# Rotary row swaps by shuffles on the vector engine instead of permutation matmuls on the tensor engine

## The reference

```python
# axial attention of the first block, 16 query heads of 64 on 4 key groups; pairs (i, i + 16) in each 32 rows
q = rms(q) * q_gain;  k = rms(k) * k_gain
q, k = rotate(q), rotate(k)            # x * cos + swap(x) * sin, of the 512 tokens, not of the context
# _mla_branch, 8 heads ("latent"): 64 plain rows and 32 rotary rows, pairs (i, i + 16); key rows shared by the heads
q_pe, k_pe = rotate(q_pe), rotate(k_pe)
# _diff_branch, 8 heads ("diff"): two queries and two keys of 64 rows, the first 16 of each turned, pairs (i, i + 8)
dq, dk = rotate(dq[:16]), rotate(dk[:16])
scores = q @ k.T;  weights = softmax(scores);  out = weights @ v
```

## Time and profile before

| | before |
|---|---|
| median of 3 runs | 4189.98 us (4186.84 to 4192.81) |
| span of the profiled execution | 4189.2 us |
| PE busy | 3968.2 us, 95% |
| DVE busy | 2070.7 us, 49% |
| ACT busy | 1490.1 us, 36% |
| POOL busy | 1630.0 us, 39% |
| mean granted TensorE clock | 0.968 |

### The profile page before, as it was taken

The page is one execution under the profiler, slowest core; times in us unless marked ns, Lnnn a source line. Parts: engine busy times, 40 slices in busy tenths (PEclk is TensorE's granted clock), DMA queues, the critical chain, the costliest instruction groups (busy, mean ns, idle before and its releaser), DMA issues.

```text
span 4189.2 us, 59665 instructions
## 1 busy us (share of the span) xinstructions
PE 3968.2 (95%) x20860; PEld 3354.5 (80%) x20860; DVE 2070.7 (49%) x3364; ACT 1490.1 (36%) x2420; POOL 1630.0 (39%) x2044
## 2 busy tenths in 40 slices
PE   7999988999988979999999999999989999999998
PEld 6788888999977767888777788788877777887887
DVE  5556655223347666225737723533367476235225
ACT  3212222111236543222646534322246456333222
POOL 1111123333421105566333245466642423555565
PEclk9899999999989989999999999999999999999999
DMA  5334211112110002322121122223221211322222
GB/s 187 125 123 144 79 51 51 61 65 64 61 46 26 21 11 93 98 98 96 56 70 57 51 86 96 76 96 100 96 66 41 81 51 61 100 86 77 99 95 96
DMA packets 92747, 328.31 MB, mean 78 GB/s; under 512 B 10240, under 2 KB 12544, under 8 KB 92544
## 3 DMA queue, kind: packets, MB, share of 16 engines
q1 hardware_dynamic: 90928, 323.61, 23.3%
q10 hardware_dynamic: 1616, 1.90, 0.2%
HBM read 323.38 MB, written 2.10 MB: 78 GB/s over the span
## 4 chain that ended last, share of the span: by engine, by line
issue 61%; POOL 30%; PE 8%; DVE 1%; POOLq 1%; ACT 0%; DVEq 0%
POOL Wl L259 30%; PE psum L1142 3%; PE psum L1143 3%; PE psum L1144 3%; POOLq L254 0%; POOLq L256 0%; DVE S L1990 0%; DVE M L2168 0%; PE psum L1209 0%; DVE X L1990 0%; DVE X L2124 0%; PE psum L1199 0%; DVE X L2185 0%; POOLq L259 0%; ACT hand L380 0%
## 5 line engine op out<-in xcount | busy, mean ns | idle before, releaser
L259 POOL TENSOR_TENSOR Wl<-raw,Wh 128x256 fp32r<-128x256 f32 x2040 | 1629.8, 829 | 2552.9 <-ACT Wh L370 2552.5
L370 ACT ACTIVATE Wh<-raw 128x1024 fp32r<-128x1024 f32 x510 | 540.0, 1059 | 1689.9 <-PE psum L1144 1664.3
L1142 PE MATMUL psum<-Hh,Wh 128*128 128x512 f32 (+1 forms) x2704 | 1037.9, 384 | 50.2 <-DVEq L2033 17.0
L1143 PE MATMUL psum<-Hl,Wh 128*128 128x512 f32 (+1 forms) x2704 | 1018.3, 377 | 0.0
L1144 PE MATMUL psum<-Hh,Wl 128*128 128x512 f32 (+1 forms) x2704 | 1017.0, 376 | 0.0
L1142 PE MATMUL psum<-Gh,Wh 128*128 128x512 f32 (+3 forms) x2032 | 751.1, 370 | 17.5 <-DVEq L2033 7.9
L1144 PE MATMUL psum<-Gh,Wl 128*128 128x512 f32 (+3 forms) x2032 | 745.7, 367 | 0.0
L1143 PE MATMUL psum<-Gl,Wh 128*128 128x512 f32 (+3 forms) x2032 | 745.3, 367 | 0.0
L1142 PEld LDWEIGHTS psum<-Hh,Wh 128*128 128x128 f32 x2704 | 520.5, 192 | 157.6 <-issue 52.1
L1144 PEld LDWEIGHTS psum<-Hh,Wl 128*128 128x128 f32 x2704 | 520.1, 192 | 71.4
L1143 PEld LDWEIGHTS psum<-Hl,Wh 128*128 128x128 f32 x2704 | 521.0, 193 | 67.9 <-issue 1.3
(11 more groups left out here) (345 smaller groups left out, 4702.9 us busy)
## 6 DMA issues: line engine op xcount, KB each, us to landing
raw<-in_wstream SPq DMA_DIRECT2D x510, 512.0 KB, 3.4
stage<-in_ada SPq DMA_DIRECT2D x80, 512.0 KB, 4.3
M<-in_ada SPq DMA_DIRECT2D x16, 512.0 KB, 5.9
X<-in_xT SPq DMA_DIRECT2D x1, 2048.0 KB, 14.1
out<-X SPq DMA_DIRECT2D x8, 256.0 KB, 2.0
X<-in_ctxT SPq DMA_DIRECT2D x1, 1024.0 KB, 9.2
M<-in_memT ACTq DMA_DIRECT2D x1, 1024.0 KB, 5.6
M<-in_axial ACTq DMA_DIRECT2D x1, 512.0 KB, 3.5
```

The lines of the kernel that those rows point to most:

```text
L259: pool.tensor_tensor(Wl[:, s, c], raw[:, s, c], Wh[:, s, c].bitcast(F32), ALU.subtract).then_inc(w_low, 1)
L370: act.activation(Wh[:, s], raw[:, s], ACT.Copy).then_inc(v["w_high"], 1)
L1142: pe.matmul(dst, a[0], b[0], start=first, stop=False)
L1143: pe.matmul(dst, a[0], b[1], start=False, stop=False)
```

## The change

The three permutation matrices are gone, and so are all 62 matmuls with them, with the PSUM tile, the bank and the wait that each took. DVE makes the swap itself, with `stream_shuffle`, which permutes the partitions inside each 32, from SBUF to SBUF; then it multiplies the result by the sine table, in SBUF too. The signs of the sine table now are zero in rows that aren't rotary, since the shuffle moves those rows as well. PE's waits for raw values move from in front of the swaps to in front of the transposes that still need them.

```diff
-CONST_COLS = 6 * P + 4
+CONST_COLS = 3 * P + 4
+SWAPPED = {n: [i ^ n for i in range(32)] for n in (8, 16)}
...
 # axial attention, PE
-    def rotated_keys():
-        pe.wait_ge(v["keys_scaled"], keys_scaled.next())
-        exact(P, SEQ, rot0, k32[:, X0:TOK])
-
-    def rotated_queries(t):
-        exact(P, SEQ, rot0, q_raw[t])
...
-                if u == 5:
-                    rotated_keys()
                 if u == 6:
-                    rotated_queries(0)
                     square_sums(1)
...
 # latent attention, PE
         if more:
-            rotated(2 if before else 3)
             keys_and_values()
-        else:
-            pe.wait_ge(v["raw_done"], counts.raw_done.next())
+        raw_values_taken(3 if h < 2 else 2)
         turned_values(h)
...
     from_tokens()
-    twin_rotated(0)
-    twin_rotated(1)
-    pe.wait_ge(v["raw_done"], counts.raw_done.next())
+    raw_values_taken(1)
     turned_values(1)
...
 # diff attention, PE
         scores(4 * h + 3)
-        if more:
-            rotated(0)
-            rotated(1)
         turned_weights(4 * h + 2)
...
 # axial attention, DVE
     def turn(x):
-        b = look()
-        tt_last(b, S0[:], psum[:, b, :], sinA, ALU.mult)
+        do(dve.stream_shuffle(S0[:], x, SWAPPED[16]))
+        tt(S0[:], S0[:], sinA, ALU.mult)
         tt(x, x, cosA, ALU.mult)
         tt(x, x, S0[:], ALU.add)
...
 # latent attention, DVE
+    swapped = v["diag"][rope].rearrange("p b q -> p (b q)")
     def rotate():
-        b = look()
-        tt(S0[rope, :], psum[rope, b, :], sinM[rope, :], ALU.mult)
-        free(b)
+        do(dve.stream_shuffle(swapped, S0[rope, :], SWAPPED[16]))
+        tt(S0[rope, :], swapped, sinM[rope, :], ALU.mult)
         tt(S0[rope, :], S0[rope, :], S1[rope, :], ALU.add)
         dve.sem_inc(v["turned_ready"], 1)
...
 # diff attention, DVE
-    def turned_part(b):
-        tt_last(b, turned, halves(psum[:, b, :]), sinD, ALU.mult)
+    def turned_part(c):
+        do(dve.stream_shuffle(turned, X[:, 2 * c:2 * c + 2, 0:CTX], SWAPPED[8]))
+        tt(turned, turned, sinD, ALU.mult)
...
         if more:
-            turned_part(look())
+            turned_part(0)
         low_weights(1, weights_bank)
         combine(4 * h + 3)
-        if more:
-            key = look()
         low_weights(2, look())
         if more:
             rotate(0)
-            turned_part(key)
+            turned_part(1)
```

More of the change, by code:

```diff
@@ L162, in build @@
         const = sb("const", [P, CONST_COLS])
-        ident, ones, bones, rot0, rot1, rot2 = (const[:, i * P:(i + 1) * P] for i in range(6))
-        groups_to_rows, heads_to_rows = const[:, 6 * P:6 * P + 2], const[:, 6 * P:6 * P + 4]
+        ident, ones, bones = (const[:, i * P:(i + 1) * P] for i in range(3))
+        groups_to_rows, heads_to_rows = const[:, 3 * P:3 * P + 2], const[:, 3 * P:3 * P + 4]
         onesr = sb("onesr", [P, P], F32R)
@@ L811, in attention_act @@
                 high_weights(u - 1)
-            if u == 0:
-                tiles.skip(1)
-                if more:
-                    keys()
+            if u == 0 and more:
+                keys()
             if u == 1 and g == 2:
@@ L1108, in pe_program @@
     psum, S0, S1, M, tab, diag, onesr = (v[n] for n in ("psum", "S0", "S1", "M", "tab", "diag", "onesr"))
-    ones, bones, ident, rot0, rot1, rot2 = (v[n] for n in ("ones", "bones", "ident", "rot0", "rot1", "rot2"))
+    ones, bones, ident = (v[n] for n in ("ones", "bones", "ident"))
     @block.tensor
@@ L1496, in attention_pe @@
 def attention_pe(pe, v, tiles, project_block, project_first, mm3, exact, counts):
-    psum, hand, ident, ones, bones, rot0 = (v[n] for n in ("psum", "hand", "ident", "ones", "bones", "rot0"))
+    psum, hand, ident, ones, bones = (v[n] for n in ("psum", "hand", "ident", "ones", "bones"))
     H, G, Ph, Pl = (v["Hh"], v["Hl"]), (v["Gh"], v["Gl"]), v["Ph"], v["Pl"]
     Qh, Ql, Kh, Kl, Vh, Vl = (v[n] for n in ("Qh", "Ql", "Kh", "Kl", "Vh", "Vl"))
-    exp, k32, k2, q_raw, q_sq, v_raw = attention_views(v)[:6]
-    keys_scaled = Count()
+    exp, _, k2, _, q_sq, v_raw = attention_views(v)[:6]
     def scores(g, u):
@@ L1605, in attention_pe @@
                 turned_weights(u - 1)
-            if u == 0:
-                rotated_queries(1)
-                if more:
-                    keys()
+            if u == 0 and more:
+                keys()
             if u == 1 and g == 2:
@@ L1632, in latent_pe @@
 def latent_pe(pe, v, tiles, weights, project_block, mm3, exact, cq, n_block, query_sums, counts):
-    psum, X, stage, S0, ident, rot1 = (v[n] for n in ("psum", "X", "stage", "S0", "ident", "rot1"))
+    psum, X, stage, ident = (v[n] for n in ("psum", "X", "stage", "ident"))
     Hh, Hl, Qh, Ql, Kh, Kl, Vh, Vl = (v[n] for n in ("Hh", "Hl", "Qh", "Ql", "Kh", "Kl", "Vh", "Vl"))
@@ L1757, in turned_weights @@
         mm.then_inc(v["tile_done"], 1)
-    def rotated(c):
-        pe.wait_ge(v["raw_done"], counts.raw_done.next())
-        exact(P, SEQ, rot2, X[:, 2 * c:2 * c + 2, 0:CTX])
     def turned_values():
         b = tiles.take(pe)
-        pe.wait_ge(v["raw_done"], counts.raw_done.next())
+        pe.wait_ge(v["raw_done"], counts.raw_done.next(3))
         for tt in range(4):
```

48 lines of the change are left out of this document (10 added, 38 removed).

## The result

The changed kernel takes 4255.09 us, median of 4 runs (4247.56 to 4261.05), against 4189.02 of the kernel before, 4 runs on the same chip: a ratio of 1.0152, 95% interval 1.014 to 1.0165. It is slower, as forecast, but by 66 us where I had 29, and outside the range of 4202 to 4245. The profiled execution took 4261.05, the slowest of the four, with a span of 4259.3.

A forecast was written before the change was run, and what follows sets the result against it. The prediction took DVE, which releases PE, as the bound in the latent, diff and most axial stretches. Diff +24.4, latent +9.4, axial +2.3 and PE-bound places -6.9 made +29.2 us, so 4219 us, range 4202 to 4245.

The forecast's parts named there:

- the sentence on the latent heads: Latent heads: 14 turns lie on DVE's path at 0.67 us each, +9.4 us; PE's saving only lengthens its wait.
- the rival of the falling clock: Diff heads: PE's longer idle time halves its clock, 4236 us if in half the heads, 4253 in all; chance 0.13.
- The price of the shuffle: Each DVE shuffle of 512 elements a partition takes 0.75 us, with bounds of 0.49 and 1.23.
- The turn's growth in a latent head: Latent heads: shuffle and wait, less an idle time no longer paid, lengthen DVE's turn by 0.67 us.
- both turns of a diff head: Diff heads: both turns lie on the chain from scores 4h+3 to low weights 3, which grows by 1.80 us.
- PE is not the bound: Whole kernel: DVE releases PE; the opposite rival, PE as bound with 53 us gained, gave 4137 us, chance 0.05.
- The diff heads: Diff heads of both layers: 12 grow by 1.8 us and two first heads by 1.4, +24.4 us in all.
- The places that PE bounds: Before the latent heads and at the hand-over of each layer: eight swaps removed at 0.86 us, -6.9 us.
- the hand-over: End of each layer's latent heads: two swaps removed from PE, 1.72 us gained a layer.
- The axial attention: Axial attention: nine turns that matter, their costs partly offset by PE's savings and an earlier free bank, +2.3 us.

The follow-up runs named there:

- two matmuls beside the shuffle: Changed kernel with the latent loop's swap matmul made twice by PE, results unread, beside the shuffle whose result is used; 4225.56 us.
- one matmul beside the shuffle: Changed kernel with the latent loop's swap matmul put back once on PE, result unread, beside the shuffle whose result is used; 4231.07 us.
- neither: Changed kernel without the shuffles too: the row swap is left out everywhere, so the rotary embedding is not the reference's; 4188.36 us.
- matmul and shuffle everywhere: Kernel before with all shuffles added and used, every swap matmul kept on PE and its result unread; 4243.72 us.
- DVE late, PE untouched: Kernel before, in the latent loop alone: DVE makes the shuffle twice and uses it, PE's swap matmul stays and is unread; 4221.18 us.
- latent shuffle alone: Kernel before with the shuffle in place of the matmul in the 14 swaps of the latent loop alone; 4218.74 us.
- diff matmuls back: Changed kernel with the 28 swaps of the diff heads made by PE's matmul again, all others by shuffle; 4219.28 us.
- the places where PE sets the pace: Changed kernel with matmuls again for all latent-loop, diff-head and axial swaps except the axial second query tile; 4180.26 us.
- latent matmuls back: Changed kernel with the 14 swaps of the latent loop made by PE's matmul again, all others by shuffle; 4215.05 us.
- the query turns moved to an early place: In diff heads DVE makes the query's whole turn before weights 4h+2's division; with shuffles where PE sets the pace, 4176.40 us, ratio 0.9965 to the kernel before.
- the step that was late next (low weights 1): The 4176.40 us version with DVE's low weights 1 moved ahead of scaling the former head's output in diff heads; 4162.59 us.

## Why the prediction missed

**The step that failed.** It is the sentence on the latent heads: "The 0.86 that PE saves a head turns into a longer wait for DVE." I let the matter rest there, and put the rival of the falling clock in the diff heads alone. The sum that I left out stands in numbers that I had: 0.87 idle before, 0.86 saved, 0.67 added to DVE, 2.40 in one piece. The trace has 2.35 where 0.88 stood before, and 2.46 where 0.99 stood. Ahead of the second head it has 3.8, which this sum doesn't give. In the diff heads I had worked out the idle times and asked what the clock would do, with pieces of 1.4, 1.2 and 2 us; in the latent heads, where the longest piece was to come, I had not. The rows in hand bracketed it: 2.09 idle in the axial attention with 12 transposes at half clock behind it, 0.87 of 3 with none. The profiled executions bear it out (a fall is counted where a head's 12 scores matmuls took 3.5 us or more instead of 2.9; idle times are those ahead of the second and third weights tiles, in one piece or two):

| profiled execution | second head's idle us | later heads' idle us | falls in 14 heads | seven heads, us |
|---|---|---|---|---|
| before | 1.05 | 0.9 to 1.0 | 0 | 97.9 |
| two matmuls beside the shuffle | 1.05 | 0.8 to 1.3 | 0 | 104.9, 104.5 |
| one matmul beside the shuffle | 1.9 | 1.1 to 1.6 | 2 | 107.2, 106.8 |
| neither | 3.0 | 1.2 to 1.7 | 2 | 98.7, 98.2 |
| matmul and shuffle everywhere | 1.9 | 1.1 to 1.6 | 2 | 105.8, 104.5 |
| DVE late, PE untouched | 1.6, 1.1 | 1.6 to 2.3 | 5 | 114.3, 113.0 |
| latent shuffle alone | 4.8, 4.4 | 1.8 to 2.5 | 9 | 109.0, 113.5 |
| changed kernel | 3.8 | 1.8 to 2.5 | 12 | 112.1, 118.0 |
| diff matmuls back | 3.8 | 1.8 to 2.1 | 14 | 118.6, 118.3 |

Among the runs whose latent heads have one shuffle each, those with the most falls have the longest stretches. What the idle time alone doesn't tell is which heads: a fall makes the next one likely. In the last three rows of the table 30 heads come right behind a slow one, and 26 of them are slow too, though PE waits only 1.79 to 2.06 us ahead of them. The cost of one fall is 3.1 - 0.6 = 2.5 us, because the scores stretch from 2.9 to 5.3 and DVE's ring hangs on them. 11 heads make 27 of the 40 us by which the profiled execution was past the forecast.

The Trainium skill ("TensorE: Matmul & The Clock Gate", section "HAM oscillation — how this bites in real kernels") describes a loop in which each trip waits, loses the clock and starts cold again. The trace agrees: from 2076.3 on the heads of layer 0 have a clock of 0.80 and a length of 17.0 or 17.1. The waits of the page's example are longer, about 3 to 5 us; here 1.8 to 2.5 us were followed by a fall in most heads, and the measurement decides. I had cited another section of that page for the diff heads, and not held the latent loop against this one.

**What was right.** The price of the shuffle: 0.75 taken, 0.747 in the diff heads, 0.725 in the latent ones. An estimate from the Trainium skill ("VectorE: DVE Perf Modes", section "The perf-mode tier table") was 0.80; the measured number decides, and is a little lower. The turn's growth in a latent head: 0.67 forecast, 0.64 measured. That both turns of a diff head lie on the chain from scores 4h+3 to `output`, with its three idle times: 12.29 measured for 12.2. That PE is not the bound: without any swap the time is that of before. That the places where PE sets the pace gain from the change: run by themselves, 4180.26 for 4180 to 4183.

**Terms that were off in size.** The diff heads: +31.5 for +24.4. Matched starts, head by head, split it. In the changed kernel and the three other runs with shuffles alone there (one and two matmuls, latent matmuls back) a diff head without a fall of the clock grew by 1.5 to 2.3 us, mostly by the 1.8 forecast, and 11 of the 17 heads with a fall by 3.1 to 3.8. Three heads of the changed kernel are of these, so some 5 of the 7 us come from the clock (0.98 and 0.97); this rival had a chance of 0.13 and came true for a small part. The places that PE bounds: -4.6 for -6.9. At the hand-over 1.8 are gained at once, as forecast, and 0.7 are lost again on the way to the diff heads, in every kernel with shuffles in place of the matmuls there; whose wait that is I did not follow. Before the latent heads the gain is there too, but PE then waits 0.61 for the first low keys, and the first head gives back 1.0 to 1.3 a layer; that is why the first heads of the loop grew by 1.9 and 1.6 instead of 0.67. The axial attention: +3.4 for +2.3, which is close by luck. The forecast's own parts are some 7.6 for the shuffles and 5.5 of gains; measured, the shuffles beside the matmuls cost 14.0, and taking the matmuls away then gains 10.6, but only 2.6 without shuffles. Why these parts don't add was not followed.

**What stays open.** Which heads catch the fall. The same heads with the same code have a mean clock of 0.88 and 0.83 in the changed kernel, 0.83 in both layers of its version with diff matmuls, and 0.92 and 0.86 with the latent shuffle alone. That the runs of the changed kernel spread over 13 us would follow from this. Their mean clocks fit, 0.957 in the fastest, 0.955 in the middle two and 0.952 in the slowest, but falls elsewhere count in these as well, and only one execution has a trace, so this is argued and not shown.

## What to carry to other kernels

When work is taken from an engine that isn't the bound, add up how long it then stands idle at a time (what it waited, what it saves, what the other engine gains), also in the first turn of a loop, and ask what its clock does with that; two matmuls whose result nobody read were worth 30 us here. An operation moved to the engine that releases the other is paid twice if the clock falls. Place by place is better than all or none: of 62 swaps, the few ahead of PE's long runs and the query turns moved to an early place were worth taking, and the step that was late next (low weights 1) gave as much again as they did together (0.9965 to 0.9931).

## What the runs showed of the hardware

- A STREAM_SHUFFLE within 32 partitions of 512 fp32 elements took 0.725 to 0.733 us over 32 partitions and 0.726 to 0.750 us over 128 (means by line of the changed kernel), with a LOAD_MASK_SELECT of 0.01 us ahead of each.
- In the latent heads of the changed kernel TensorE's clock fell to 1.2 GHz in 12 of 14 heads. Ahead of the falls it had stood idle for 3.8 us (2 heads), 2.46 us (1) or, right behind a head that had fallen, 1.79 to 1.95 us (9). It held behind 1.93 and 2.35 us. In the run with neither matmul nor shuffle it held behind 1.58 to 1.71 us in ten heads; with both everywhere it fell in two heads behind 1.5 us in two pieces.
- A head at 1.2 GHz in its scores took 17.0 us instead of 14.5.
- Giving TensorE useless fp32 matmuls made the kernel faster: 4255.09 to 4231.07 us with one a head, 4225.56 with two.
